# First expert layer: four rows per partition in the down weights, and a weight ring of five 16 KB slots

## What is computed

```
def swiglu(h, w_in, w_out):
    gate, up = jnp.split(h @ w_in, 2, axis=-1)
    return (jax.nn.silu(gate) * up) @ w_out

def moe_swiglu(h, router, w_in, w_out):
    logits = (hf @ router).astype(jnp.float32)
    top_logit, top_idx = lax.top_k(logits, TOP_K)          # 2 of 8
    top_w = jax.nn.softmax(top_logit, axis=-1)
    gates = jnp.einsum('nk,nke->ne', top_w, jax.nn.one_hot(top_idx, N_EXPERTS))
    for e in range(N_EXPERTS):
        y = y + gates[:, e:e + 1] * swiglu(hf, w_in[e], w_out[e])
```

## Time and profile before

| | us |
|---|---|
| three runs, median | 1953.35 (1952.22 to 1957.31) |
| the profiled execution | 1952.21 |
| its span, first to last instruction | 1950.3 |
| first weight DMA of the first expert layer issued | 626.66 |
| first matmul on these weights | 649.6 |
| last matmul of the last down step ends | 1489.3 |
| granted TensorE clock over the span, mean | 0.962 |

### The profile page before, as it was taken

The page is one execution under the profiler, slowest core; times in us unless marked ns, Lnnn a source line. Parts: engine busy times, 40 slices in busy tenths (PEclk is TensorE's granted clock), DMA queues, the critical chain, the costliest instruction groups (busy, mean ns, idle before and its releaser), DMA issues.

```text
span 1950.3 us, 26935 instructions
## 1 busy us (share of the span) xinstructions
PE 1803.6 (92%) x11133; PEld 1026.3 (53%) x11133; DVE 609.2 (31%) x1248; ACT 474.7 (24%) x797; POOL 356.6 (18%) x307
## 2 busy tenths in 40 slices
PE   8999999999987899999999999999996887699996
PEld 7987999777965333323332333223232786544442
DVE  6777555338475200100010000000002686500111
ACT  5854434325421110000100000001001564322120
POOL 3000000000000699999920000000000201000000
PEclk9998999998998799999999999999998898799998
DMA  6545666447625999999999999999995640589995
GB/s 191 157 136 200 199 206 216 152 131 249 195 87 196 395 400 386 420 420 420 416 420 420 420 416 418 420 420 419 418 419 218 181 134 31 216 321 420 419 419 232
DMA packets 152744, 582.93 MB, mean 299 GB/s; under 512 B 11673, under 2 KB 77866, under 8 KB 109600
## 3 DMA queue, kind: packets, MB, share of 16 engines
q1 hardware_dynamic: 150000, 575.09, 75.8%
q0 software_dynamic: 2608, 5.97, 1.2%
HBM read 579.96 MB, written 1.05 MB: 298 GB/s over the span
## 4 chain that ended last, share of the span: by engine, by line
PE 44%; DMA 14%; DVE 6%; ACT 2%; issue 1%; DVEq 0%; SPq 0%; ACTq 0%
PE ps L1765 16%; DMA ring<-in_moe_w_out 10%; PE ps L2200 6%; PE ps L1758 4%; PE ps L1797 4%; PE ps L2224 3%; DMA ring<-in_moe_w_in 3%; PE ps L1801 1%; DMA more<-in_moe_w_in 1%; PE ps L2167 1%; PE ps L2185 1%; PE ps L436 1%; PE ps L2168 1%; PE ps L438 1%; PE ps L437 1%
## 5 line engine op out<-in xcount | busy, mean ns | idle before, releaser
L1765 PE MATMUL ps<-ring,xg 128*64 128x512 f32 x1638 | 407.2, 600 | 5.5 <-DMA ring<-in_moe_w_in 2.6
L472 DVE TENSOR_TENSOR wlo<-raw,whi 128x2048 fp32r<-128x2048 f32 (+5 forms) x96 | 211.5, 2206 | 190.6 <-ACT whi L464 190.3
L1765 PEld LDWEIGHTS ps<-ring,xg 128*64 128x64 f32 x1638 | 121.4, 137 | 249.1 <-issue 239.9
L464 ACT ACTIVATE whi<-raw 128x2048 fp32r<-128x2048 f32 (+6 forms) x97 | 178.8, 1846 | 187.2 <-PE ps L438 70.9
L436 PE MATMUL ps<-xh,whi 128*128 128x272 f32 (+1 forms) x712 | 210.4, 295 | 1.2 <-DVE xl L521 1.2
L438 PE MATMUL ps<-xh,wlo 128*128 128x272 f32 (+1 forms) x712 | 208.5, 293 | 0.0
L1797 PE MATMUL ps<-ring,ahm 128*64 128x512 f32 x808 | 202.9, 597 | 5.9 <-DMA ring<-in_moe_w_out 5.8
L437 PE MATMUL ps<-xl,whi 128*128 128x272 f32 (+1 forms) x712 | 208.3, 293 | 0.0
L2133 POOL TENSOR_SCALAR lnt<-lnt,h 128x384 f32<-128x384 f32 x120 | 188.5, 1571 | 12.2
L1935 DVE TENSOR_TENSOR sgm<-sgm,ps 128x512 f32<-128x512 f32 x28 | 17.4, 682 | 501.1 <-PE ps L1765 501.1
L742 POOL DMA_DIRECT2D lnt<-in_ln_gain x4 | 2.2, 559 | 799.7 <-issue 513.8
(11 more groups left out here) (581 smaller groups left out, 2422.9 us busy)
## 6 DMA issues: line engine op xcount, KB each, us to landing
ring<-in_moe_w_in SPq DMA_DIRECT2D x117, 1024.0 KB, 19.6
ring<-in_moe_w_out SPq DMA_DIRECT2D x101, 1024.0 KB, 19.9
ring<-in_moe_w_in SPq DMA_DIRECT2D x117, 768.0 KB, 11.8
ring<-in_w_gate SPq DMA_DIRECT2D x29, 1024.0 KB, 13.6
raw<-in_ffn_w_in SPq DMA_DIRECT2D x28, 1024.0 KB
ring<-in_w_down SPq DMA_DIRECT2D x26, 1024.0 KB, 13.0
raw<-in_w_ada SPq DMA_DIRECT2D x24, 1024.0 KB
ring<-in_w_up SPq DMA_DIRECT2D x20, 1024.0 KB, 11.9
```

The lines of the kernel that those rows point to most:

```text
L464: e.activation(whi[0:rows, s % NSPL, 0:n], raw[0:rows, i % NRAW, 0:n], ACT.Copy).then_inc(S.hi.s, S.hi.up((s,)))
L472: e.tensor_tensor(wlo[0:rows, s % NSPL, 0:n], raw[0:rows, i % NRAW, 0:n], whi[0:rows, s % NSPL, 0:n].bitcast(F32), ALU.subtract).then_inc( ...
L1765: ins = e.matmul(ps_[b][64 * v:64 * v + 64, :], a[:, j, 64 * v:64 * v + 64], both[v][:, 0, 512 * b:512 * b + 512], start=j == 0, stop=j == 7)
```

## The change

`w_out` is loaded with four rows per partition: one DMA brings 512 rows of one expert (2 MB, 16 KB per partition), and serves two of the old down steps. The ring has five slots of 16 KB in the place of eleven of 8 KB (`more1` is gone, 8 KB per partition less). A slot is now a *unit* (`home`): in the up steps the two experts' pieces of one step share one slot (and its semaphore), one at offset 0 and one at 8 KB; in the down steps each expert's 2 MB piece has a slot of its own. SP waits once per unit for TensorE's mark of the unit five before. In `down` TensorE waits at even `j` for both experts' units and marks them as used behind odd `j`. The transposes read `sgm` and `sgo` with a step of four floats, and so does `quarter` the ring. The number of matmuls and the bytes loaded stay the same.

```
-NRING1, NMORE1, CAP_A, CAP_B = 11, 1, 96, 64
+NRING1, CAP_A, CAP_B = 5, 96, 64
...
-                part = lambda v: w_out[bass.ds(v, 1), 256 * j:256 * j + 256, :].rearrange("e (p k) n -> p (e k) n", p=128)
-                m = 2
+                part = lambda v: w_out[bass.ds(v, 1), 512 * j:512 * j + 512, :].rearrange("e (p k) n -> p (e k) n", p=128)
+                m = 4
...
-            w = CW if nm == "d" else n
+            w = 2 * CW if nm == "d" else n
...
+            S.home.append((unit[0], CW * u if nm != "d" else 0))
...
-            steps += [("d", 0, j) for j in range(14)]
+            steps += [("d", 0, j) for j in range(7)]
             for s in steps:
                 for u in range(2):
+                    unit[0] += s[0] == "d" or u == 0
                     chunk(x, u, *s)
...
+    ring2 = ring.rearrange("p (a b) n -> p a (b n)", b=2)
...
-            if i >= NRING1:
-                e.wait_ge(C.pe.s, C.pe.at("ring", C.S.name, i - NRING1))
+            if unit != seen and unit >= NRING1:
+                e.wait_ge(C.pe.s, C.pe.at("ring", C.S.name, unit - NRING1))
...
-                v = w["sgm"][:, b, :].rearrange("p (j q i) -> p j i q", j=2, i=2)
+                v = w["sgm"][:, b, :].rearrange("p (q i) -> p i q", i=4)
...
-            return a[:, 512 * c:512 * c + 512] if n == 2048 else a.rearrange("p (s j q i) -> p j i s q", j=2, q=128, i=2)[:, c // 2, c % 2]
+            return a[:, 512 * c:512 * c + 512] if n == 2048 else a.rearrange("p (s q i) -> p i s q", q=128, i=4)[:, c]
...
-                both = pair_weights(e, C, SLOTS1, (key, x, "d", 0, j), 2)
+                if j % 2 == 0:
+                    four = first_weights(e, C, (key, x, "d", 0, j // 2), 4)
+                both = [a[:, 2 * (j % 2):2 * (j % 2) + 2] for a in four]
...
-                ins.then_inc(C.pe.s, C.pe.up(*pair_used(C, (key, x, "d", 0, j)), (key, "D", x)))
+                ins.then_inc(C.pe.s, C.pe.up(*(first_used(C, (key, x, "d", 0, j // 2)) if j % 2 else ()), (key, "D", x)))
```

More of the change, by code:

```diff
@@ L125, in __init__ @@
         self.chunks, self.split, self.index, self.stop, self.kept = [], [], {}, None, set()
+        self.home = []
     def add(self, key, rows, n, pieces, split=True, zero=False, keep=False):
@@ L261, in chunk @@
                 part = lambda v: w_in[bass.ds(v, 1), 128 * j:128 * j + 128, o:o + n].rearrange("e (k p) n -> p (e k) n", p=128)
-            w = CW if nm == "d" else n
+            w = 2 * CW if nm == "d" else n
             pieces = lambda s, v: [(s[:, 0:w].rearrange("p (k n) -> p k n", k=m), part(v))]
+            S.home.append((unit[0], CW * u if nm != "d" else 0))
             S.add((key, x, nm, gi, j, u), 128, w, pieces, split=False)
+        unit = [S.home[-1][0] if S.home else -1]
         for x in range(NP1):
             steps = [(nm, gi, j) for gi in range(len(GROUPS)) for nm in "gu" for j in range(8)]
-            steps += [("d", 0, j) for j in range(14)]
+            steps += [("d", 0, j) for j in range(7)]
             for s in steps:
                 for u in range(2):
+                    unit[0] += s[0] == "d" or u == 0
                     chunk(x, u, *s)
@@ L1551, in ring_slots @@
         return out + [(a, ((pe, end), (act, end), (dve, end))) for a in more]
-    SLOTS1 = ring_slots("go", first, [more1[:, i, :] for i in range(NMORE1)], "end_gla")
+    ring2 = ring.rearrange("p (a b) n -> p a (b n)", b=2)
+    free1 = {a.offset: before for a, before in ring_slots("go", first, [], "end_gla")}
+    SLOTS1 = [(ring2[:, k, :], free1[ring[:, 2 * k, :].offset] + free1[ring[:, 2 * k + 1, :].offset]) for k in (0, 1, 2, 3, 4)]
     def load_ring(e, C, slots, main):
@@ L1567, in load_first @@
     def load_first(e, C, main):
-        place = {}
+        place, seen = {}, -1
         for i, ((key, x, _, _, _, u), _, _, pieces, _, _) in enumerate(C.S.chunks):
-            slot, before = SLOTS1[i % NRING1]
-            if i >= NRING1:
-                e.wait_ge(C.pe.s, C.pe.at("ring", C.S.name, i - NRING1))
-            elif main:
+            unit, o = C.S.home[i]
+            k = unit % NRING1
+            slot, before = SLOTS1[k]
+            if unit != seen and unit >= NRING1:
+                e.wait_ge(C.pe.s, C.pe.at("ring", C.S.name, unit - NRING1))
+            elif unit != seen and main:
                 for sig, *mark in before:
                     e.wait_ge(sig.s, sig.at(*mark))
+            seen = unit
             s = 2 * x + u
@@ L1581, in load_first, with first_weights, first_used @@
                 place[key, s] = 0 if Sig.counting else v
-            for dst, src in pieces(slot, place[key, s]):
-                e.dma_start(dst, src).then_inc(C.S.raw[i % NRING1].s, C.S.raw[i % NRING1].up((i,), by=16))
+            for dst, src in pieces(slot[:, o:], place[key, s]):
+                e.dma_start(dst, src).then_inc(C.S.raw[k].s, C.S.raw[k].up((unit,), by=16))
+    def first_weights(e, C, key, m):
+        both = []
+        for u in range(2):
+            i = C.S.index[(*key, u)]
+            unit, o = C.S.home[i]
+            n = C.S.chunks[i][2]
+            if u == 0 or unit != C.S.home[i - 1][0]:
+                e.wait_ge(C.S.raw[unit % NRING1].s, C.S.raw[unit % NRING1].at(unit))
+            both.append(SLOTS1[unit % NRING1][0][:, o:o + n].rearrange("p (k n) -> p k n", k=m))
+        return both
+    def first_used(C, key):
+        return [("ring", C.S.name, C.S.home[C.S.index[(*key, u)]][0]) for u in range(2)]
     def pair_weights(e, C, slots, key, m):
@@ L1693, in turn @@
             for i in range(n // 512):
-                a = w["sgo"][:, 256 * (i // 2):256 * (i // 2) + 256] if n == 2048 else w["sgo"][:, 128 * i:128 * i + 128]
-                ins = e.transpose(p[:, 128 * i:128 * i + 128], a.rearrange("p (q i) -> p i q", i=2)[:, i % 2, :] if n == 2048 else a, idn)
+                a = w["sgo"].rearrange("p (q i) -> p i q", i=4)[:, i, :] if n == 2048 else w["sgo"][:, 128 * i:128 * i + 128]
+                ins = e.transpose(p[:, 128 * i:128 * i + 128], a, idn)
             ins.then_inc(C.pe.s, C.pe.up((key, "turno", x, gi)))
@@ L1752, in up @@
                     for j in range(8):
-                        both = pair_weights(e, C, SLOTS1, (key, x, nm, gi, j), 1)
+                        both = first_weights(e, C, (key, x, nm, gi, j), 1)
                         for what in ("mo", "om")[j % 2]:
```

5 lines of the change are left out of this document (2 added, 3 removed).

## The result

| | before | after |
|---|---|---|
| median of 4 runs each, us | 1953.89 (1952.22 to 1957.31) | 1987.43 (1979.69 to 1993.98) |
| ratio, 95% interval | | 1.0168 (1.0129 to 1.0207) |
| profiled execution, span, us | 1950.3 | 1985.9 |
| first weight DMA of the layer to the end of its last down matmul | 862.6 | 892.3 |
| from there to the end | 461.1 | 469.3 |

The forecast was 1965 with a range from 1956 to 1976; the changed kernel takes 33 us more than before, 1.7%. Its time is that of rival D (1988), which had a chance of 0.07. Most of the loss lies in the expert layer.

The account below looks back on a forecast made before the run. DMA was taken to set the pace, with only 6 us of slack on TensorE per pair. The terms -5.0 + 4.2 + 1.9 + 4.4 + 7.6 = +13.1 us on 1952.2 gave 1965 us, range 1956 to 1976.

Parts of the forecast that it names:

- rival D: Narrow up group: the four-float read halves the speed of L1758, +36 us in all, 1988 us; chance 0.07.
- Part 6: Matmul count, DMA issues, transposes and the moving read at a step of four floats: no cost, 0 us.
- Part 4: First down unit of each pair: `turn` delays the release, lead 3.6 us, 1.1 us lost four times, +4.4 us.
- Part 1: `w_out` loads: 2 MB DMAs of 16 KB pieces take 4.89 us where two took 4.98, -5.0 us.
- The need of 4.7 us: DMA queue: time needed from a DMA's issue to the landing of the one before it, or the stream loses time.
- the bounds of the need alone: Whole kernel: the uncertainty in the queue lead needed was said to reach from 1957 to 1975 us.
- C: Rival: the steady down steps starve of DMAs too; priced at 1975 us, 1982 at a need of 6.0; chance 0.12.
- Part 5: Narrow up group, second and third pair: TensorE arrives late, lead 0.9 us, 3.8 us lost in each, +7.6 us.
- E: Rival: longer `w_out` pieces save more, 2 MB landing every 4.5 us, -9 us, 1943 us; chance 0.08.
- F: Rival: the long pieces bring nothing, being cut to 8 KB on the way, +18.1 us, 1970 us; chance 0.10.
- Part 2: End of the down product: two steps instead of one run behind the last landing, +4.2 us.
- Part 3: First pair: ten 8 KB pieces instead of eleven lie ahead, so the stream is one DMA behind, +1.9 us.

Follow-up runs that it names:

- the read alone: The kernel before with only the further tokens' read in the narrow up group at a step of four floats: 1967.9 us, ratio 1.0075.
- ring-alone kernel: The changed kernel with the narrow group's read for the further tokens back at a step of two floats: 1979.1 us, ratio 1.0123.
- ring of five with old pieces: The changed kernel's five 16 KB slots, but `w_out` in two rows per partition (1 MB DMAs) and the reads of before: 1960.5 us, ratio 1.0017.

## Why the prediction was wrong

**Part 6, the moving read, is the step that failed.** I wrote of L1758 "Between 0 and a doubling (rival D) I take 0, from the weight loads." The weight loads of the transposes did behave as said, 209 ns also with the step of four (min/median/max):

```profile
L1718 PEld LDWEIGHTS ps<-cst,sgo x28: 139/209/209, 734.1 to 1454.2; 128*128 128x128 f32 x28
```

But they are no neighbour of a moving operand. 16 matmuls went from 1.49 to 2.82 us, D's doubling within a tenth. D's sum was too high, though: it had 12 us in the first pair and 6 in each other, together 30; the read alone gives +15, and by pairs of the traces 6.3, 4.5, 4.4 and -2.3. In the narrow step 0.28 us are lost to the load rate and 0.38 taken from slack, and much of what TensorE falls behind it makes up in the down steps. D's 1988 was right by luck, by two errors that cancel: the read dearer in its sum than in the run, the ring cheaper.

**Part 4, the first down unit, was mis-sized: 12 us and not 4.4.** The four down parts took 287.2 us in the ring-alone kernel and 279.9 and 280.2 in the two traces of before; that is +7.2, and with part 1's -5 +12. The lead at the first release was 1.0, 0.8, 0.4 and 1.3 us and not 3.6, and 11.2 us were lost there. The release came 13.5 us behind the landing and not the 11 that "two steps, 8.88 us", 0.2 and the turn make: the step I priced from the earlier trace rows began there at half the clock, behind 6 us in which TensorE had idled. The idle time itself was in my working (both units must have landed), its effect on the clock was not. The need of 4.7 us was too high at this place, which made up for a part of it: lead and loss together were 3.5 to 3.8 us there, and with 4.7 the same leads would have cost 15. Nor do "the bounds of the need alone" end at 1975, as I wrote: with a need of 6.0 my own sum is C's 1982.

**Part 5, the narrow group, was right in kind; that its size fits is in part luck.** Predicted +7.6; both narrow groups took 131.5 us in the ring-alone kernel, 121.8 and 123.8 in before: +8 to +10. That TensorE brings its lateness along from the down part, and that the fourth pair is spared, both showed. Not right was that one loss fills the queue again: in the second pair the DMAs of 949.5, 950.0, 955.6 and 956.2 lost 1.4, 0.7, 1.6 and 0.8 us more than 1.89, in turn. The shortest lead was 2.7 us there and 2.3 in the third pair, not 0.9: several small losses came to the size of the one that I had summed up.

**Part 1 was right.** 2 MB land every 4.9 us wherever the queue is deep. In the ring-alone kernel the landings 823.14 + 10.20 and 842.74 + 10.21, four DMAs apart, lie 19.6 us apart, 4.90 us each and not 4.89:

```profile
823.14 10.20 DMA ring<-in_moe_w_out
...
842.74 10.21 DMA ring<-in_moe_w_out
```

E and F fall with it. **Part 2 was right**: TensorE ends 9.2 us behind the last landing and not 4.8, +4.4 for +4.2. **Part 3** was +1.9 and is +2.7 in the ring-alone kernel's landings of the first pair's up part; the ring of five with old pieces has +2.5. **C is out**: of 16 steady releases in the down parts, at leads of 4.4 to 5.9 us, 13 lost nothing and three 0.4 to 0.6 us.

The ring's part by its terms: -5.0 + 4.4 (end) + 2.7 (first pair) + 12.2 (first unit) + 8.7 (narrow) + 0.6 (the rest) = 23.6, and layer 886.9 less the mean of before, 863.2, is 23.7. The first and the fourth term are measured only together, as +7.2; the rest is the wide groups of the later pairs, +1.6, and the narrow one of the fourth, -1.0. In after the two causes don't simply add: 892.3 is only 5.4 over it in the layer (some 9 in the timed runs). With the slow read TensorE is never early at the down start: it begins 0.9 to 1.5 us behind the landing in all four pairs. In the second pair its windows from 1000 to 1030 us have clock 1.00, and the first half takes 3.43 us in the chain:

```profile
1015.71 3.43 PE ps L1822 x16
```

So one disturbance seems to cover the other; no run tests that by itself.

What nobody undid is the first pair's +2.7 us. And no version here beats before: outside the first pair its queue is full and its TensorE work hidden, so the 5 us of longer pieces were about all that this change could gain.

## What to carry to other kernels

Price an access pattern by the operand that it reads: that a step of four floats costs a weight load no more than a step of two says nothing of the moving operand, where here one float of each 16 bytes took 851 ns and two took 507. When transfers are made longer, the gain per byte is small (some 5 us here), while three costs grow with the piece: the wait for the first one, the work that is left behind the last one, and the lag that goes with it into the next stage; lag decays only by the difference of the two rates, here 0.54 us a step. And an idle time of TensorE of several us is not only idle time: look at the granted clock of the windows behind it before taking a step's price from a row in full flow.

## What the runs showed of the hardware

- A 128x384 matmul of 32 columns' stationary, four side by side: 494, 507, 682, 851 and 864 ns at a step of 1, 2, 3, 4 and 8 floats of the moving operand. Weight loads of 128x128: 142 ns contiguous, 209 ns at 2 and at 4.
- In a wait of TensorE from 785.5 to 791.5 us the granted clock was 0.51 between 789 and 791, 0.50 up to 795 while it worked again, and 1.00 from 797 us: a wait of 6 us made the next 3.6 us of work 5.8. With 18 added matmuls in the wait, 2.1 to 2.4 us of it were left in three pairs and the same work took 5.3 to 5.4 us; in the pair where 0.9 us were left it took 3.7.
- DMAs of 2 MB in one queue, lead and loss of the four first releases: 1.0 and 2.8 us, 0.8 and 2.7, 0.4 and 3.3, 1.3 and 2.5; at leads of 4.4 to 5.9 us 13 of 16 lost nothing.
- The stretch behind the layer takes 461 to 470 us in traces of kernels that are the same there.
